# Two-block denoising step on one core: gate products among the low norms, the rotation beside the query products, the output in parts

## What is computed

```python
for l in range(2):                                  # second block
    a_lat = x_lat * (1 + sc1) + sh1                 # 256 x 1024
    f, nq, nk, nv, cq, ckv, kr, g = split(a_lat @ w_in[l])
    y_f   = fourier_mix(f)
    y_na  = neighbourhood_attention(nq, nk, nv, context keys, ...)
    q     = concat(rms_norm(cq) @ w_uq, axial_rope(rms_norm(cq) @ w_qr))   # 8 heads, 64 + 32
    k     = concat(rms_norm(ckv) @ w_uk, axial_rope(kr) for every head)
    v     = rms_norm(ckv) @ w_uv
    y_mla = softmax_attend(q, concat(context k, k), concat(context v, v))
    m_lat = sum over b of sigmoid(g[b]) * (y[b] @ w_branch[b])  @ w_out
    x_lat = layer_norm(ALPHA * x_lat + (1 + g1) * m_lat)
    f_lat = (silu(h @ w_gate) * (h @ w_up)) @ w_down            # h: modulated x_lat, hidden 2816
    x_lat = layer_norm(ALPHA * x_lat + (1 + g2) * f_lat)
return x_lat
```

## Time and profile before

| | |
|---|---|
| median of 3 runs | 3045.1 us (3044.39 to 3056.07) |
| the profiled execution | 3047.46 us |
| its span, first to last instruction | 3045.7 us |
| mean granted TensorE clock | 0.952 |
| TensorE products busy | 2736.5 us, 90% of the span |
| weight loads of TensorE | 1856.9 us, 61% |
| VectorE, ScalarE, GpSimd busy | 788.7, 453.7, 74.8 us |
| read from memory | 759.20 MB, 250 GB/s over the span |

### The profile page before, as it was taken

One profiled execution on the slowest core, in us unless ns is written; L12 is line 12 of the kernel. 1 busy time (PEld: TensorE's weight loads), 2 busy tenths in 40 slices (PEclk: granted clock), 3 DMA queues, 4 the chain that ended last, 5 costly groups with the idle time before them and its releaser, 6 DMA issues.

```text
span 3045.7 us, 33992 instructions
## 1 busy us (share of the span) xinstructions
PE 2736.5 (90%) x13754; PEld 1856.9 (61%) x13754; DVE 788.7 (26%) x1893; ACT 453.7 (15%) x971; POOL 74.8 (2%) x144
## 2 busy tenths in 40 slices
PE   6998987889989969899999598898999897998998
PEld 2554544446567845555554356587788544687886
DVE  1344202221121261111111414414642224313002
ACT  2132002121120021000000113301000122301000
POOL 0000000000000000000000000000000000000000
PEclk9998998899999979999999799999999999999999
DMA  9874998999966519999999432143675211133330
GB/s 397 330 328 185 372 413 350 383 421 410 422 279 262 197 64 400 422 411 422 419 422 422 165 120 77 56 148 129 258 283 205 111 55 56 74 148 135 142 138 14
DMA packets 117580, 764.86 MB, mean 251 GB/s; under 512 B 12784, under 2 KB 15600, under 8 KB 34224
## 3 DMA queue, kind: packets, MB, share of 16 engines
q1 hardware_dynamic: 94352, 680.57, 55.3%
q0 software_dynamic: 20224, 74.26, 6.2%
q10 hardware_dynamic: 2848, 7.83, 0.6%
HBM read 759.20 MB, written 3.41 MB: 250 GB/s over the span
## 4 chain that ended last, share of the span: by engine, by line
PE 75%; DMA 14%; DVE 6%; issue 2%; ACT 2%; SPq 1%; POOL 0%; ACTq 0%; DVEq 0%
PE bank L542 73%; DMA ring<-in_stream 13%; PE bank L841 1%; PE bank L830 1%; SPq L422 1%; DMA work<-in_stream 1%; PE bank L546 1%; DVE work L1835 1%; DVE MX L1897 0%; ACT work L1432 0%; DVE work L1914 0%; DVE work L1694 0%; DVE work L1687 0%; DVE work L2349 0%; DVE X L2114 0%
## 5 line engine op out<-in xcount | busy, mean ns | idle before, releaser
L542 PE MATMUL bank<-A,ring 128*128 128x256 f32 (+1 forms) x3088 | 712.0, 390 | 17.7 <-issue 7.7
L542 PEld LDWEIGHTS bank<-A,ring 128*128 128x128 f32 x3088 | 588.8, 191 | 134.8 <-issue 43.7
L542 PE MATMUL bank<-ring,A 128*32 128x512 f32 (+3 forms) x2304 | 418.4, 638 | 82.3 <-DMA ring<-in_stream 71.4
L542 PE MATMUL bank<-work,ring 128*128 128x256 f32 x1696 | 386.5, 386 | 8.8 <-DVE work L1843 6.1
L542 PEld LDWEIGHTS bank<-work,ring 128*128 128x128 f32 x1696 | 326.0, 193 | 61.2 <-DVE work L1843 7.6
L542 PE MATMUL bank<-work 128*64 128x128 f32 (+5 forms) x2084 | 338.5, 332 | 14.9 <-DVE work L1772 5.2
L542 PEld LDWEIGHTS bank<-ring,A 128*32 128x32 f32 (+2 forms) x2304 | 127.9, 129 | 355.3 <-issue 228.1
L542 PE MATMUL bank<-A,work 128*128 128x256 f32 x1280 | 292.9, 386 | 20.0 <-ACT A L1330 11.4
L542 PEld LDWEIGHTS bank<-work 128*128 128x128 f32 (+2 forms) x2084 | 247.4, 172 | 79.2 <-issue 44.5
L542 PEld LDWEIGHTS bank<-A,work 128*128 128x128 f32 x1280 | 242.5, 192 | 79.5 <-issue 33.6
L542 PE MATMUL bank<-work,par_sb 128*128 128x256 f32 (+2 forms) x228 | 82.4, 500 | 75.7 <-ACT work L1432 23.0
(11 more groups left out here) (266 smaller groups left out, 1506.4 us busy)
## 6 DMA issues: line engine op xcount, KB each, us to landing
ring<-in_stream SPq DMA_DIRECT2D x648, 1024.0 KB, 12.6
work<-in_stream POOLq DMA_DIRECT2D x134, 512.0 KB, 8.7
X<-in_xt ACTq DMA_DIRECT2D x1, 2048.0 KB, 13.9
spill<-work ACTq DMA_DIRECT2D x3, 512.0 KB, 9.9
work<-spill POOLq DMA_DIRECT2D x3, 512.0 KB, 4.9
tab_sb<-in_tab_a ACTq DMA_DIRECT2D x1, 1120.0 KB, 18.6
X<-in_ctx2t ACTq DMA_DIRECT2D x1, 1024.0 KB, 15.5
out<-X SPq DMA_DIRECT2D x1, 1024.0 KB, 4.8
```

The source lines that it names most:

```text
L542: return pay(pe.matmul(o, w, x, start=start, stop=stop, tile_position=place), tells)
```

## The change

1. Of the merge's 24 gate products of a layer the first two (`EARLY`) are made among the low norms: the first between the sum of squares of `cq` and that of `ckv`, the second between the latter and `krope`. Their sigmoids go to a place of their own, `SGE`; the merge then starts with two branch products.
2. The rotation's product of a head stands two query products (`QLAG`) behind its own query product, ahead of the keys and values. VectorE rotates the queries before it copies the key's rotation and the values.
3. VectorE's work for the second layer's modulation (L2380 to L2385 before) goes between the fifth and the sixth `down` product's step of layer 0.
4. The output leaves in four transfers of two chunks, each as soon as its chunks are ready.

```diff
+EARLY, QLAG = 2, 2
 def lin_order():
-        out += one(f"low{l}", "DDDD") + one(f"krope{l}", "D") + one(f"mq{l}", "A" * 8) + one(f"mk{l}", "A" * 8)
-        out += one(f"mv{l}", "D" * n) + one(f"qrope{l}", "D" * 8)
-        out += one(f"merge{l}", "ADADAD" * KD) + one(f"out{l}", "D" * KD) + one(f"up{l}", "AD" * KF)
+        merge = one(f"merge{l}", "ADADAD" * KD)
+        early = [merge[2 * i] for i in range(EARLY)]
+        out += one(f"low{l}", "DDDD") + early + one(f"krope{l}", "D")
+        for j in range(8 + QLAG):
+            out += [(f"mq{l}", j, "A")] if j < 8 else []
+            out += [(f"qrope{l}", j - QLAG, "D")] if j >= QLAG else []
+        out += one(f"mk{l}", "A" * 8) + one(f"mv{l}", "D" * n)
+        out += [x for x in merge if x not in early] + one(f"out{l}", "D" * KD) + one(f"up{l}", "AD" * KF)
...
+        SGE = wk(16384, EARLY, T)
...
-            sp.wait_ge(norm_out, NOUT["ln2_1"] + KD)
-            sp.dma_start(out, X[:, :, 0:T]).then_inc(out_sent, 16)
-            sp.wait_ge(out_sent, 16)
+            for k in range(0, KD, 2):
+                sp.wait_ge(norm_out, NOUT["ln2_1"] + k + 2)
+                sp.dma_start(out[:, k:k + 2, :], X[:, k:k + 2, 0:T]).then_inc(out_sent, 16)
+            sp.wait_ge(out_sent, 64)
...
                 norm(f"cq{l}", w)
+                linear(f"merge{l}", 0, w, lambda k: tile(f"l{l}_merge", k), lambda k: A[:, k, 0:w], KD)
                 norm(f"ckv{l}", kw)
+                linear(f"merge{l}", 2, w, lambda k: tile(f"l{l}_merge", 12 + k), lambda k: A[:, k, 0:w], KD)
...
-                for j in range(8):
-                    linear(f"mq{l}", j, w, lambda k: tile(st, 2 * j + k), lambda k: LOW[:, k, 0:w], 2)
+                for j in range(8 + QLAG):
+                    if j < 8:
+                        linear(f"mq{l}", j, w, lambda k: tile(st, 2 * j + k), lambda k: LOW[:, k, 0:w], 2)
+                    if j >= QLAG:
+                        wait_taken(pe, f"mq{l}", j - QLAG)
+                        linear(f"qrope{l}", j - QLAG, T, lambda k: tab(TC, "swap"), lambda k: A[:, j - QLAG, 0:T], 1)
...
-                for j in range(8):
-                    wait_taken(pe, f"mq{l}", j)
-                    linear(f"qrope{l}", j, T, lambda k: tab(TC, "swap"), lambda k: A[:, j, 0:T], 1)
-                last_taken(pe, f"qrope{l}")
+                last_taken(pe, f"mv{l}")
...
-                        linear(f"merge{l}", j, w, lambda k: tile(st, at + k), lambda k: A[:, k, 0:w], KD,
-                               wait=(lambda k: pe.wait_ge(a_again, KD * l + k + 1)) if j == 0 else None)
+                        if j >= 2 * EARLY:
+                            linear(f"merge{l}", j, w, lambda k: tile(st, at + k), lambda k: A[:, k, 0:w], KD,
+                                   wait=(lambda k: pe.wait_ge(a_again, KD * l + k + 1)) if j == 2 * EARLY else None)
...
                 squares(f"ckv{l}", kw, lambda k: LOW[:, 2, 0:kw])
+                for j in range(EARLY):
+                    act.activation(SGE[:, j, :], take(f"merge{l}", 2 * j, w), ACT.Sigmoid).then_inc(taken["A"], 1)
...
-                for j in range(3 * KD):
-                    if j >= 2:
+                for j in range(EARLY, 3 * KD):
+                    if j >= EARLY + 2:
...
-            def outer(l, stage, gate, w):
+            def outer(l, stage, gate, w, ahead=None):
                 for j in range(KD):
+                    if ahead and j == 5:
+                        ahead()
...
-                for h in range(HEADS):
-                    dve.tensor_copy(MK[rot, h, 0:kw], LOW[rot, 3, 0:kw]).then_inc(kr_copied, 1)
-                for j in range(kw // P):
-                    dve.tensor_copy(V2[:, j, :], take(f"mv{l}", j, 512)).then_inc(taken["D"], 1)
                 for j in range(8):
                     wait_taken(dve, f"mq{l}", j)
...
+                for h in range(HEADS):
+                    dve.tensor_copy(MK[rot, h, 0:kw], LOW[rot, 3, 0:kw]).then_inc(kr_copied, 1)
+                for j in range(kw // P):
+                    dve.tensor_copy(V2[:, j, :], take(f"mv{l}", j, 512)).then_inc(taken["D"], 1)
...
-                        s = SG[:, (o * 3 + b) % 2, 0:w]
+                        s = SG[:, (o * 3 + b) % 2, 0:w] if o * 3 + b >= EARLY else SGE[:, b, 0:w]
...
-                outer(l, f"down{l}", 40, w)
-                if l == 0:
+                def second_mods():
                     take_mods(3, 0, 5, 0, 12)
                     plus_one(1, 0, 16)
                     plus_one(1, 16, NMOD, 1)
                     for k in range(KD):
                         dve.tensor_scalar(A[:, k, T:2 * T], X[:, k, T:2 * T], MODP[:, 1, 8 + k, 1:2], MOD[:, 3, k, 1:2],
                                           ALU.mult, ALU.add).then_inc(ctx_a_ready, 1)
+                outer(l, f"down{l}", 40, w, None if l else second_mods)
```

## The result

The changed kernel took 3009.69 us (median of 4, 3007.24 to 3010.92) where the kernel before took 3046.5 (median of 4, 3044.39 to 3056.07): a ratio of 0.9872 with a 95% interval of 0.9857 to 0.9888, 1.3% faster. The forecast was 3005, its range 2999 to 3017. The profiled execution took 3007.24 us with a span of 3005.4, 40.3 less than before, at a mean granted clock of 0.958 (0.952 before).

A forecast was written before the change was run, and what follows sets the result against it. TensorE was taken as the bound. Layer 0 15.9, layer 1 17.8, norm 4.2 and output 2.2 made 40.1 us off the profiled 3047.5: 3007.4, or 3005 for the median, range 2999 to 3017.

The forecast's parts named there:

- attention starts earlier: Low norms to attention: early gates and interleaved rotation start the attention 6.2 us earlier in layer 0, 8.6 in layer 1.
- warm start of the attention: First score products of the attention: less idleness ahead raises the clock, saving 2.3 us in layer 0, 1.8 in layer 1.
- merge, two gates and its start: Merge: two gate products leave it, 6.9 us a layer, and its start saves 0.5 a layer.
- norm behind `down` of layer 0: Second block's modulations move under the down products: 4.2 us saved, 2.4 of work and 1.8 of clock.
- output: End of the kernel: four transfers instead of one, last landing 2.55 us after its issue, 2.2 saved, bounds 0 and 3.0.
- The gates: Low norms: two gates fill TensorE's idle time; queries start 0.4 us later in layer 0, 1.0 earlier in layer 1.
- The rotation: Query start to attention: rotation woven among queries takes 17.4 us in layer 0, 21.7 in layer 1; VectorE keeps up.
- the wait of the keys: Layer 0: key product 3 waits 0.9 us for the last rotation's bank; no such wait in layer 1.
- the slower rival: Attention falls to 1.2 GHz and stays there, costing 44 us: 3049, slower than before; chance 0.02.
- The rival that the clock does not rise: Queries, first scores and norm: the clock parts, 10.8 us together, fail to come, giving 3016; chance 0.15.
- The merge's start: Branch products in front leave only the attention's copy to wait for: 0.5 us a layer; either layer may win or lose 1.7.

The follow-up runs named there:

- e6: Changed kernel with a third early gate product behind the second; 2999.60 us, one run.
- e2: Kernel before with only the two early gate products, the rotation staying behind the values; 3033.96 us, ratio 0.9947.
- e7: Changed kernel with the first two key products woven between the last rotation products; 3000.19 us, one run.
- e3: Kernel before with only the rotation products moved beside the query products, no early gates; 3032.39 us, ratio 0.9938.
- e8: Changed kernel with each rotation product directly behind its own query product; 3014.48 us, one run.
- e5: Kernel before with useless products in TensorE's idle time at the low norms and ahead of the attention, nothing moved; 3040.61 us, ratio 0.9984.
- e1: Kernel before with only the moved modulation work and the output in four transfers; 3040.76 us against 3050.47, ratio 0.9959.
- e4: Changed kernel with useless products in TensorE's idle time of three norms (behind both merges and layer 0's `down`); 2998.97 us, ratio 0.9824.
- e9: Changed kernel with the output in eight transfers of one chunk; 2999.68 us, one run.
- e12: The changed kernel unedited, run again; 3006.15 us (6 runs) against 3052.98, ratio 0.9840.

## Why the prediction was right

The mechanisms were right, one by one, and seven of the eight terms held to 0.3 us each, the output to 0.45; that the whole execution came out at 40.3 against 40.1 is in part luck, since 5.3 us that no term had were won and 4.9 were lost. Point by point, by its own terms, in us of the profiled execution:

| term | predicted | measured |
|---|---|---|
| layer 0: attention starts earlier | 6.2 | 6.1 |
| layer 0: warm start of the attention | 2.3 | 2.2 |
| layer 0: merge, two gates and its start | 7.4 | 7.4 (and 1.7 more, not in the sum) |
| layer 1: attention starts earlier | 8.6 | 8.3 |
| layer 1: warm start of the attention | 1.8 | 1.7 |
| layer 1: merge, two gates and its start | 7.4 | 7.4 |
| norm behind `down` of layer 0 | 4.2 | 4.2 |
| output | 2.2 | 2.65 |
| sum | 40.1 | 39.9 |

**1. The gates.** The queries of layer 0 start 0.48 later (0.4 predicted). In layer 1 they start 0.72 earlier instead of 1.0: the sum of 512 columns ends later than the full-speed 0.86 would have it. The timeline of the kernel after has 1.16 us from its start to the square root:

```profile
2530.28 1.12 PE L552 MATMUL bank<-work,par_sb 128*128 128x512 f32 x2 [0.70 <-ACT work L1446]
...
2531.44 0.69 ACT L1448 ACTIVATE work<-bank,EPS 128x512 f32<-128x512 f32 x1 [1.22 <-PE bank L552]
...
2536.36 2.86 PE L552 MATMUL bank<-work,ring 128*128 128x256 f32 x12 [1.07 <-DVE work L1859]
```

A lone pair of instructions takes 0.3 more than the price from the long groups of the merge gives (1.12 for the row itself, 0.86 by that price); the step left this fixed part out. The table load (L1640) is there, 1.28 us, with nobody behind it. e6 shows what a gate costs without cover, e2 that the two gates are free.

**2. The rotation.** 17.41 and 21.71 against 17.4 and 21.7, of which 1.0 was an estimate; the wait of the keys, 0.9 predicted, was two waits of the weight loads, together 1.2, of which e7 gave 0.86 back. e3 bears out that VectorE keeps up, e8 that the two heads of distance cover ScalarE's copy.

**3. The attention's start** is warm in both layers, and it stays so: over the 30 us behind it the table by stretch of the kernel after has

```profile
1908.00:1938.00 30.00, 26.86 (x196) 15.87 (x194) 18.81 (x55) 18.35 (x42) 0.00 (x0) 1.00 0.19 71
```

so the slower rival (0.02) fell. The rival that the clock does not rise (0.15) fell in these executions: queries, scores and the norm behind `down` ran at 2.4 GHz. e5 shows the clock part by itself, 8.3 us.

**4. The merge's start** gave its 0.5. That layer 0 might win 1.7 more stood in the prediction as left open; it did, and losses elsewhere ate it.

**5. The norm** gave 4.16 of 4.2, in e1 alone 4.15.

**6. The output.** The first issue comes 12.43 after the last residual, when two chunks are ready; the last comes at 3002.78, 14.82 after it, just where the single issue stood before. So the whole gain is the landing of the last part: 2.3 behind its issue, where 2.55 was worked out, instead of 4.8. An issue took 0.38 and not the 0.68 of the prediction, which changed nothing, because the parts come every 0.80. The Trainium skill's page "DMA: Bandwidth & Descriptors" (Anatomy of one DMA — SWDGE (gpsimd) path) gives a fixed cost of about 2.0 us for a transfer issued from GpSimd's queue. By that figure and the 0.75 of the transfer itself the estimate for the last part would be 2.75. The output here is issued by SyncE, and its landings, 2.3 and 2.0 us for 256 and 128 KB, fit a smaller fixed cost; no run here shows GpSimd's queue by itself.

**The sum and the median.** The sum held to 0.2 us. The median fell 4.7 above the forecast: 1.4 because the kernel before now has a median of 3046.5 instead of 3045.1, 3.3 because the medians differ by 36.8 and the profiled executions by 40.2. Where that lies isn't shown, since only one execution of each is profiled, and that of the kernel after was the fastest of its four. The stretch ahead of the low norms could hold it: it differs by up to 14 us between the profiled executions here. Where the prediction was incomplete is the norms behind `out`: it treated stages that the diff doesn't touch as unchanged, and 4.9 us were lost there and in the `ffn` products behind them. It left 1.7 us open for the merge starts only.

**What decides that loss** is only half settled. It is clock: the granted clock is 0.59 in the slow norm, and e4 takes the loss away and more with useless products. It isn't tied to the change: the norm behind `out` of layer 0 takes 14.15 in e1 too, whose TensorE code there is that of the kernel before, and 12.17 in e9, whose code there is that of the kernel after. The Trainium skill's page "TensorE: Matmul & The Clock Gate" (Part 1) says that the same kernel comes out differently from run to run, because the monitor's window is free-running. This case agrees in part: two executions of one program differ at the start of block 2 (3.62 or 5.32 us for the same 26 instructions, e12), and then agree in every stage from the low norms on. Why the slow norm came in both of them and not in e9 stays open; two executions can't tell a habit of the program from chance.

## What to carry to other kernels

Price each edit of an engine-bound stretch by the idle time ahead of the bound engine's rows and by the granted clock behind it, since 8 us here were clock alone (e5); a gap of 2 to 5 us ahead of TensorE cost its own length and then some 2 us more, and one of 1.3 or 1.4 us did so in some executions. Fill such gaps with real products if there are any, and with useless ones if not (10 us here, e4); but expect stages that you didn't touch to change by steps of 1 to 2 us, from one execution to the next too, and judge by stages, since the total hides them. A merged row of the timeline holds the idle time between its instructions: take the duration of one from the view of its line. When products are woven with work of other engines, leave a distance between a product and the one that needs its copy; two products between were enough here, and with none the wait for the copies cost 11 us.

## What the runs showed of the hardware that I had not expected

- SyncE was held by an issue of the output for 0.38 us with 256 KB, for 0.45 with 128 KB back to back, and for 0.68 with 1 MB: cutting a store finer didn't make its issues shorter.
- The same 16 instructions behind the same 1.43 us of idleness take either 4.93 or 6.92 us (granted clock 1.00 or 0.59). Two executions of one program agreed in this, and differed by the same kind of step elsewhere (3.62 or 5.32 us, granted clock 1.00 or 0.50).
- TensorE can be at half speed while busy: after 3.94 and 2.02 us of idleness e3's query products ran for 4.2 us at a granted clock of 0.50 with no further idle time, and the next 4.0 us had a mean of 0.81.
